# A mixture of experts on one core: six of eight items written out ahead of the loop, and VectorE transposing the hidden blocks

## What is computed

```python
def moe_swiglu(hn, router_w, w_gate, w_up, w_down):      # top 2 of 8 experts, width 3584
    logits = (xt @ router_w).astype(jnp.float32)
    top_logit, top_idx = lax.top_k(logits, TOP_K)
    gate = jax.nn.softmax(top_logit, axis=-1)
    ...
    def expert_block(args):
        xblk, e = args
        return (jax.nn.silu(xblk @ w_gate[e]) * (xblk @ w_up[e])) @ w_down[e]
```

## Time and profile before

| | |
|---|---|
| median of 3 runs | 1506.87 us (1506.83 to 1508.54) |
| the profiled execution | 1508.99 us, of which its span 1506.9 us |
| TensorE busy | 1444.1 us, 96% of the span |
| mixture of experts, first up product to last down product | 527 to 1495 us |
| mean granted TensorE clock | 0.977 of full speed |

### The profile page before, as it was taken

How to read it: one execution, slowest core, us unless ns; L and a number is a source line. 1 busy time by engine, 2 the same in 40 slices (tenths; PEclk the granted TensorE clock), 3 DMA queues, 4 the chain that set the end, 5 groups by cost and what they waited for, 6 DMA issues and landing times.

```text
span 1506.9 us, 37207 instructions
## 1 busy us (share of the span) xinstructions
PE 1444.1 (96%) x16771; PEld 854.9 (57%) x16771; DVE 389.7 (26%) x809; ACT 295.8 (20%) x556; POOL 100.1 (7%) x82
## 2 busy tenths in 40 slices
PE   6999999999999899989999998998998999999997
PEld 6998859999996534534533443453453444344444
DVE  5765445555454340110101001001011010100102
ACT  5631234444464100100100001000010010000111
POOL 4330010000000000010000001001001000100100
PEclk9999999999999899999999999999999999999999
DMA  7531127565634569999998998998999899899992
GB/s 274 205 116 57 59 70 232 168 194 195 218 117 168 193 260 407 415 403 366 382 386 328 387 378 325 382 406 301 386 398 371 339 381 384 326 385 380 397 368 85
DMA packets 146885, 436.78 MB, mean 290 GB/s; under 512 B 5544, under 2 KB 31072, under 8 KB 146608
## 3 DMA queue, kind: packets, MB, share of 16 engines
q1 hardware_dynamic: 140096, 423.64, 73.5%
q0 software_dynamic: 4624, 7.42, 2.2%
q10 hardware_dynamic: 2016, 3.38, 0.7%
HBM read 427.46 MB, written 6.96 MB: 288 GB/s over the span
## 4 chain that ended last, share of the span: by engine, by line
PE 94%; issue 3%; DVE 2%; ACT 1%; DMA 1%; POOL 0%; POOLq 0%; DVEq 0%; ACTq 0%
PE bank L2151 34%; PE bank L2195 19%; PE bank L1612 6%; PE bank L1613 6%; PE bank L1614 6%; PE bank L2170 6%; PE bank L2181 2%; PE bank L2032 2%; PE bank L1838 2%; PE bank L1648 2%; PE bank L2105 1%; PE bank L1753 1%; PE bank L1736 1%; PE bank L2018 1%; DMA weights<-in_a_w_in 1%
## 5 line engine op out<-in xcount | busy, mean ns | idle before, releaser
L2151 PE MATMUL bank<-ring,xt 128*32 128x512 f32 x4608 | 513.9, 606 | 0.6 <-DVE xt L1470 0.6
L2151 PEld LDWEIGHTS bank<-ring,xt 128*32 128x32 f32 x4608 | 147.1, 112 | 347.4 <-issue 345.2
L2195 PE MATMUL bank<-ring,ws 128*32 128x256 f32 x5376 | 296.1, 379 | 0.4 <-DVE ws L1480 0.4
L2195 PEld LDWEIGHTS bank<-ring,ws 128*32 128x32 f32 x5376 | 171.0, 110 | 128.0 <-issue 13.9
L1475 DVE TENSOR_TENSOR ws<-ws,bank 64x512 f32<-64x512 f32 (+1 forms) x96 | 58.8, 613 | 538.2 <-ACT ws L939 537.9
L939 ACT ACTIVATE ws<-bank 64x512 f32<-64x512 f32 (+1 forms) x96 | 51.9, 541 | 567.2 <-PE bank L2151 492.0
L1612 PE MATMUL bank<-x_hi,weights_hi 128*128 128x256 f32 x320 | 90.3, 282 | 1.3 <-issue 1.3
L1613 PE MATMUL bank<-x_lo,weights_hi 128*128 128x256 f32 x320 | 90.2, 282 | 0.0
L1614 PE MATMUL bank<-x_hi,weights_lo 128*128 128x256 f32 x320 | 89.4, 279 | 0.0
L1480 DVE COPY ws<-bank 128x256 f32<-128x256 f32 (+1 forms) x32 | 12.5, 392 | 278.5 <-PE bank L2181 278.5
L2170 PE MATMUL bank<-ring,xt 128*32 128x256 f32 x1536 | 84.5, 380 | 0.0
(11 more groups left out here) (338 smaller groups left out, 1478.0 us busy)
## 6 DMA issues: line engine op xcount, KB each, us to landing
ring<-in_moe_w_gate SPq DMA_DIRECT2D x56, 2048.0 KB, 13.3
ring<-in_moe_w_up SPq DMA_DIRECT2D x56, 2048.0 KB, 12.3
ring<-in_moe_w_down SPq DMA_DIRECT2D x56, 2048.0 KB, 13.5
weights<-in_a_w_in SPq DMA_DIRECT2D x7, 2048.0 KB, 8.7
weights<-in_ffn_w_up SPq DMA_DIRECT2D x11, 1024.0 KB, 5.4
weights<-in_ffn_w_gate SPq DMA_DIRECT2D x11, 1024.0 KB, 5.3
weights<-in_ffn_w_down SPq DMA_DIRECT2D x11, 1024.0 KB
weights<-in_a_w_out SPq DMA_DIRECT2D x2, 2048.0 KB, 7.9
```

What stands on the lines that cost most here:

```text
L2151: m = pe.matmul(bank[b][LANE * g:LANE * g + LANE, :], xe[:, 4 * hf + kt, LANE * b:LANE * b + LANE], w[:, kt, (g % 2) * 512:(g % 2) * 512 + ...
L2195: m = pe.matmul(bank[3 + b // 2][LANE * q:LANE * q + LANE, (b % 2) * 256:(b % 2) * 256 + 256], hT[:, b, col, LANE * half:LANE * half + LAN ...
```

## The change

- Items 0 to 5 are written out in Python on PE, DVE, ACT and SP, with expert i for item i; the loop begins at item 6 (`Fori(E - 2, n_more)`) and the last item is written out as before. An item in excess now stands before expert 7, which is always the last; the plan in VectorE is longer for it (106 linked instructions instead of 77). GpSimd keeps its loop over all items.
- The engines read `n_item` after item 5; SP's loads of items 0 to 5 don't wait for the plan.
- `e_turn` goes. `e_up` reads its moving operand in runs of 32 columns out of every 64, and VectorE transposes each product block by 32x32 into one of two `hT` buffers: two transposes of 64x256 for each of three blocks of a step (64x128 in the short step). The copies from PSUM (`e_turned`) go on both engines.
- The item's short down product and its `item_out` now stand at the start of the next item.
- The next item's rows are gathered by three indirect DMAs of 128 quarter rows. `slots` loses the two matmuls for whole rows; `turn_rows` has six transposes of 128x128 instead of eight of 96x128. `Pm` goes: `first_gather` reads `Pq`, and `slots(0)` stands before the first up product.

```diff
@@ sync
+            sp.sem_inc(m_d, 1)
...
-            sp.wait_ge(s_items, 1)
-            n_more = sp.value_load(n_item[0:1, 0:1], min_val=E - 1, max_val=ITEMS - 1)
+            for i in range(E - 2):
+                e_loads(i, i)
+                e_next(i, i, i + 1)
+            sp.wait_ge(s_items, 1)
+            n_more = sp.value_load(n_item[0:1, 0:1], min_val=E - 1, max_val=ITEMS - 1)
-            with sp.Fori(0, n_more) as i:
+            with sp.Fori(E - 2, n_more) as i:
...
-            e_loads(n_more, e)
+            e_loads(n_more, E - 1)
...
@@ gpsimd
-                pool.indirect_dma_start(out=xg_e, out_offset=None, in_=xn_rows[:, :],
-                                        in_offset=bass.IndirectOffsetOnAxis(ap=slot_row[0:BLOCK, 0:1], axis=0),
-                                        compute_op=ALU.bypass).then_inc(m_rows, 16)
+                for b in range(3):
+                    pool.indirect_dma_start(out=xg_e[:, b, :], out_offset=None, in_=xn_quarters[:, :],
+                                            in_offset=bass.IndirectOffsetOnAxis(ap=quarter_row[0][:, b:b + 1], axis=0),
+                                            compute_op=ALU.bypass).then_inc(m_rows, 16)
@@ vector
-            def e_hidden(s, n=512):
+            def e_hidden(s, k, n=512, first=False):
+                def turned(b):
+                    dve.wait_ge(m_hid, s * 3 + (b + 1))
+                    blocks = e_hid[0:C, b, 0:n].rearrange("p (j u l) -> p u j l", u=2, l=LANE)
+                    for u in range(2):
+                        dve.transpose(hT[k][C * u:C * u + C, b, 0:n // 2].rearrange("p (j l) -> p j l", l=LANE),
+                                      blocks[:, u]).then_inc(m_hT, 1)
                 for b in range(3):
                     dve.wait_ge(m_act, s * 3 + (b + 1))
+                    if not first:
+                        dve.wait_ge(m_hT, s * 6 + (2 * b - 4))
                     dve.tensor_tensor(e_hid[0:C, b, 0:n], e_act[0:C, b, 0:n], bank[b][0:C, 0:n],
                                       ALU.mult).then_inc(m_hid, 1)
+                    if b:
+                        turned(b - 1)
+                turned(2)
...
             gathered(0)
+            slots(0)
...
             dve.tensor_copy(n_item[0:1, :], nover[0:1, :]).then_inc(s_items, 1)
+            e_hidden(0, 0, first=True)
+            for i in range(E - 2):
+                item(i, first=i == 0)
             dve.wait_ge(s_items, 1)
@@ tensor
-                                              w[:, kt, (g % 2) * 512:(g % 2) * 512 + 512],
+                                              in_lane(r4[(ku, kg)[g // 2]][:, kt, :], g % 2),
...
-            def item(i, last):
+            def item(i, last=False, first=False):
                 s0 = i * 4
-                e_turn(s0)
+                if not first:
+                    e_down(i - 1, 20, s0 - 1, 1, stop=True)
                 e_up(i, 0, s0 + 1)
                 pe.wait_ge(m_free, i + 1)
-                e_down(i, 4, s0, start=True)
-                e_turn(s0 + 1)
-                if last:
-                    turn_lanes(0)
-                else:
+                e_down(i, 4, s0, 0, start=True)
+                if not last:
                     slots(i + 1)
                 e_up(i, 6, s0 + 2)
-                e_down(i, 10, s0 + 1)
-                e_turn(s0 + 2)
+                e_down(i, 10, s0 + 1, 1)
                 if last:
-                    turn_lanes(1)
+                    turn_lanes()
                 e_up_last(i, 12, s0 + 3)
                 if not last:
                     turn_rows(i)
-                e_down(i, 14, s0 + 2)
+                e_down(i, 14, s0 + 2, 0)
                 if not last:
                     pe.wait_ge(m_X, i * 2 + 4)
-                e_turn(s0 + 3, 2)
-                if not last:
                     e_up(i, 16, s0 + 4)
-                e_down(i, 20, s0 + 3, stop=True)
...
             first_gather()
+            slots(0)
             pe.wait_ge(m_X, 2)
             e_up(0, -5, 0, first=True)
-            slots(0)
+            for i in range(E - 2):
+                item(i, first=i == 0)
             pe.wait_ge(s_items, 1)
             n_more = pe.value_load(n_item[0:1, 0:1], min_val=E - 1, max_val=ITEMS - 1)
-            with pe.Fori(0, n_more) as i:
-                item(i, False)
-            item(n_more, True)
+            with pe.Fori(E - 2, n_more) as i:
+                item(i)
+            item(n_more, last=True)
+            e_down(n_more, 20, n_more * 4 + 3, 1, stop=True)
             scatter(n_more)
```

More of the change, by code:

```diff
@@ L310, in trunk @@
         pos = view(sm, 508, NT, 8)
[L311 to L315, removed]
+        over = view(sm, 784, 2 * E + 1)
+        rank = view(sm, 712, 2 * E + 1)
+        ohk = view(sm, 732, 2 * E + 1)
+        oh8 = view(sm, 752, E)
+        shift = view(sm, 762, OVER + 1)
         w_next, w_now = view(sm, 776, 3), view(sm, 780, 3)
+        nx1, nx2 = view(sm, 804, 1), view(sm, 805, 1)
         tmp8 = view(sm, 548, NT, 8)
@@ L468, in _, with e_load @@
             load(1, g8[1], cols(ins["b_w_o"][0], 512, 512), s_qmm, 2)
-            def e_load(k, dst, src, free, count, turn=False):
+            def e_load(k, dst, src, free, count):
                 sp.wait_ge(free, count)
-                if turn:
+                if not isinstance(count, int):
                     sp.sem_inc(m_turn, 1)
@@ L1392, in _ @@
             link(dve.memset(wcur, 0.0))
+            link(dve.memset(over, 1.0))
             def top_two(t):
@@ L1498, in item_out, with item @@
                     dve.tensor_scalar(ye[:, 2, :], bank[4][:, 0:256], w_now[:, 2:3], None, ALU.mult).then_inc(m_y, 1)
-            def item(i, last):
+            def item(i, last=False, first=False):
                 s0 = i * 4
-                e_turned(s0)
+                if not first:
+                    item_out(i - 1)
                 if not last:
                     one_hot(i + 1)
-                e_hidden(s0 + 1)
-                e_turned(s0 + 1)
+                e_hidden(s0 + 1, 1)
                 if not last:
@@ L1509, in item @@
                     slots(i + 1)
[L1510 to L1512 removed]
+                e_hidden(s0 + 2, 0)
+                e_hidden(s0 + 3, 1, 256)
                 if not last:
                     gathered(i + 1)
[L1515 to L1518 removed]
+                    e_hidden(s0 + 4, 0)
             gathered(0)
+            slots(0)
             link(dve.tensor_copy(cnt, bank[3][:, 0:8]))
@@ L1524, in _ @@
                 link(dve.tensor_scalar(over[:, k * E:(k + 1) * E], cnt, float((k + 1) * BLOCK), None, ALU.is_gt))
-            link(dve.tensor_reduce(nover, over, AX.X, ALU.add))
-            for k in range(1, 2 * E):
+            link(dve.tensor_reduce(nover, over[:, 0:2 * E], AX.X, ALU.add))
+            for k in range(1, 2 * E + 1):
                 link(dve.tensor_tensor(rank[:, k:k + 1], rank[:, k - 1:k], over[:, k - 1:k], ALU.add))
@@ L1530, in _ @@
             link(dve.tensor_copy(wi[:, :, 1:9], wgt))
-            for k in range(OVER):
+            for k in range(OVER + 1):
+                c = E - 1 + k
                 link(dve.tensor_scalar(ohk, rank, float(k), None, ALU.is_equal))
@@ L1546, in _ @@
             dve.tensor_copy(n_item[0:1, :], nover[0:1, :]).then_inc(s_items, 1)
+            e_hidden(0, 0, first=True)
+            for i in range(E - 2):
+                item(i, first=i == 0)
             dve.wait_ge(s_items, 1)
             n_more = dve.value_load(n_item[0:1, 0:1], min_val=E - 1, max_val=ITEMS - 1)
-            e_hidden(0)
-            slots(0)
-            with dve.Fori(0, n_more) as i:
-                link.loop(i, 2)
-                item(i, False)
-            link.end(n_more)
-            item(n_more, True)
+            with dve.Fori(E - 2, n_more) as i:
+                link.loop(i - (E - 2), 2)
+                item(i)
+            link.end(n_more - (E - 2))
+            item(n_more, last=True)
+            item_out(n_more, True)
             scattered(n_more + 1)
```

224 lines of the change are left out of this document (95 added, 129 removed).

## The result

The kernel after the change takes 1444.14 us (median of 4 runs, 1443.37 to 1446.57) beside 1507.7 before in runs on the same chip: ratio 0.958, interval 0.9564 to 0.9597. That is faster by 63.6 us where the prediction had 74.4, inside its range, 12 us above its centre. The upper part of that range was there for late weights. The profiled execution took 1446.57 us and is compared with 1434.6, the sum made against the profiled execution of before.

What follows compares the result with a forecast made beforehand. TensorE, 94% of the chain, was taken to bound the kernel, with DMA close behind. Gaps 29.9, half clock 14.5, turns 28.3 and slots 3.0 less 1.3 at the start save 74.4 us: 1506.87 to 1432.5, range 1424 to 1456.

Steps and rivals of the forecast that it cites:

- The sum: Whole kernel: 29.9 + 14.5 + 28.3 + 3.0 - 1.3 = 74.4 us saved, giving 1432.5 us; chance 0.80 with small terms either way.
- Gaps 29.9 and half clock 14.5: Loop's six turns back: idle TensorE gaps (29.9 us) and slow up products behind them (14.5 us) go.
- Turns 28.3 and slots 3.0: TensorE's turns of the product blocks go, 28.3 us; the four whole-row matmuls in slots go, 3.0 us.
- Transposes 0.4 us, hidden: VectorE's six transposes per step: 0.4 us each, covered by TensorE's down product, costing zero.
- Strided reads 0: Gate and up matmuls reading runs of 32 columns: no cost; a slower rival (1544 us) had chance 0.04.
- Entering the loop 0: Reading the loop's bound and entering the loop at item 6: taken as 0, at most 7.4 us.
- Start: Before item 0: TensorE starts it at 552.0 instead of 550.73, a cost of 1.3 us, between -1 and +5.
- Item 111.2 us: One item's time on TensorE after the change, down from 122.79 us.
- Granted clock 1.00 from first to last: TensorE behind 553 us: a sign of being right, full granted clock throughout.
- DMA under this, "Zero, but narrowly": Weight loads: DMA needs 110.2 to 111.7 us per item against TensorE's 111.2, so waits for weights cost zero.
- 17 us of lag: Ring of seven weight chunks: DMA may fall some 17 us behind over the kernel; 8 x 0.5 = 4 used.
- weights late: Rival on the DMA rate: at 390 GB/s an item needs 115.4 us, kernel 1449 us (1473 at 380); chance 0.09.

Runs made afterwards that it cites:

- aligned: The kernel after with `ws`, the buffer of four ring tiles, moved back to offset 111616, a multiple of 512: 1431.3 us, ratio 0.9486.
- unroll_alone: The kernel before with only items 0 to 5 written out on all four engines, SP's loads of them not waiting for the plan: 1467.3 us, ratio 0.9722.
- looped2: The kernel after with items 0 and 1 written out and its loop from item 2 on every engine: 1456.4 us, ratio 0.9647.
- looped: The kernel after with only item 0 written out and its loop from item 1 on every engine: 1493.1 us, ratio 0.9895.

## Why the prediction was right, and where it failed

**The sum** stands: its kernel without a wait for weights was to take 1432.5 us, and `aligned`, which has none, takes 1431.3. Step by step:

- Gaps 29.9 and half clock 14.5: right. No issue of 5 us is left in after, and `unroll_alone` is 41 us faster, with another 8 us lost to a clock that the sum didn't know of. I had taken the half clock as the gap's doing alone. In `unroll_alone` it also came without a gap, behind turn and slots together. That it did no harm in the changed kernel is luck: the turns went for another reason.
- Turns 28.3 and slots 3.0: right. From `unroll_alone` to `aligned` are 36.0 us. Of the 28.3, 3.7 are the six turns at half clock, which `unroll_alone` has back already, so 24.6 + 3.0 - 1.3 = 26.3 of the sum were left to gain, and with the 8.4 of clock that go with the turns it is 34.7.
- Transposes 0.4 us, hidden: right at 402 ns. Strided reads 0: right, up products take 20.60 to 20.74. Entering the loop 0: right.
- Start: the first load of item 0 went out at 542.78 (539.3 forecast), the plan ended at 553.74 (550.6) and TensorE began item 0 at 554.8 (552.0). The row below explains most of it: `first_gather` began at 524.49, in `aligned` at 521.04, in before at 520.03. From there to item 0 it is 30.3 and 30.9 us, and 32.0 by my steps. In that one execution the front of the kernel ran 3 to 4 us longer; in `aligned` item 0 begins at 551.93.

The timeline of after at the start (start, us, engine, line):

```profile
524.49 6.53 PE L2099 MATMUL bank<-ws,xn 128*128 128x96 f32 x32 [1.41 <-DVE ws L1427]
...
530.86 1.43 PE L2108 MATMUL bank<-ws 128*128 128x2 f32 x12
...
542.78 0.38 SPq L473 DMA_DIRECT2D ring<-in_moe_w_gate  x1
```

- Item 111.2 us: measured 110.93.
- Granted clock 1.00 from first to last: not quite. It is 0.50 behind the last wait for a chunk, 3.0 us.

**DMA under this, "Zero, but narrowly": this step failed.** It was put at nothing and cost 12.9 us (1444.14 - 1431.3). Two terms of it were off. First, the rate: I took the 414 and the traffic of before as given, listed what the change does to GpSimd's transfers, and didn't ask where its new tiles and constants put the old ones. The need came out at 110.2 to 111.7 us per item and was 112.5. Second, the slack: 17 us of lag were to be allowed; with 1.6 us short per item the first wait came after five items, at about 8. The time in flight grows as the queue falls behind (18 to 24 us for 13), so the slack that a landing of 13 us leaves isn't all there to be used. And a wait, once long enough, costs clock as well, for which the step had no term. The rival "weights late" had the mechanism and the sign right (1449 at 390 GB/s); it happened at 400, with the cause unnamed. Its chance of 0.09 was too small: by its own sum the need's upper end (111.7) already lay 0.5 us over the item (111.2). Its other figure is added up wrong: by 125.8 us an item the time comes to 1432 + 8 x 14.6 - 17 = 1532, not 1529, which changes nothing else.

The parts of after's 12.0 us over the sum: 2.8 at the start, 8.5 from there to the last down product (877.1 for 868.6), 0.7 in the end part. Of the 8.5, the waits and their clock are 11.6, and the items' 0.27 x 7 and smaller terms give 3.1 back.

## What to carry to other kernels

A small tile or constant that goes, or comes, moves everything allocated behind it: where a kernel draws near its DMA rate, compare the offsets of the large DMA destinations in both versions, and pin them to a multiple of 512, which ran at the full rate in every run here. When a compute saving brings the time per item to within a few per cent of bytes over saturated rate, the forecast needs the rate to 1%, measured in windows clear of other transfers, and a chance for both outcomes. The price of a loop's turn is to be read for that loop in that place, with the loads of the instruction queue beside its gaps. Where small matmuls stand together, look at the granted clock behind them.

## What the hardware showed

- With the buffer of four ring tiles 448 bytes behind a multiple of 512, 2 MiB chunks came at 408 to 410 GB/s instead of 419, in two kernels; 128 behind, in the other buffer, cost nothing to be seen.
- A jump back cost 5.4 to 6.9 us (`looped2`), about 8.0 (before) or 11.5 to 12.1 (`looped`). Each gap of these traces goes with one or two loads of 16 KB on the instruction queue: 14 of 14 gaps with one in the looped kernels, 6 of 6 with two in before.
- In `unroll_alone`, after 2.7 us of narrow matmuls, the granted clock fell to 0.50 for 3.4 us at 5 of 7 places, though TensorE never stood still; in before it fell at none of seven such places.
- A wait of 3.6 us for a chunk brought the granted clock down to 0.50 and made the next up product 3.0 us longer; waits of about 1 us did not.
- Two gathers of 128 pieces of 1 KB fewer in each item brought 6 us over the kernel, where their bytes make 4.5: not told apart.
